# A fourth pair of split buffers for the experts, and five weight pieces of each small expert multiplied in fp32 without a split

## The reference

```
def swiglu(x, w1, w3, w2):
    return (jax.nn.silu(x @ w1) * (x @ w3)) @ w2

def moe_swiglu(x, router_w, w1, w3, w2):
    logits = (t @ router_w)
    top_v, top_i = lax.top_k(logits, TOP_K)          # 2 of 8 experts for each token
    gates = jax.nn.softmax(top_v, axis=-1)
    ...
    for e in range(N_EXPERTS):
        out = out + combine[:, e:e + 1] * swiglu(t, w1[e], w3[e], w2[e])
```

## Time and profile before

| | us |
|---|---|
| median of 3 runs | 2150.57 (2148.72 to 2155.72) |
| the profiled execution | 2145.45 |
| its span in the profile | 2143.6 |
| PE, DVE, ACT busy in it | 1996.8, 1512.1, 1102.2 |
| the eight experts, first to last piece on PE | some 728 to 1781 |

### The profile page before, as it was taken

One profiled execution on the slowest core, in us unless ns is written; L12 is line 12 of the kernel. 1 busy time (PEld: TensorE's weight loads), 2 busy tenths in 40 slices (PEclk: granted clock), 3 DMA queues, 4 the chain that ended last, 5 costly groups with the idle time before them and its releaser, 6 DMA issues.

```text
span 2143.6 us, 25381 instructions
## 1 busy us (share of the span) xinstructions
PE 1996.8 (93%) x9950; PEld 1561.8 (73%) x9950; DVE 1512.1 (71%) x1834; ACT 1102.2 (51%) x1144; POOL 58.2 (3%) x64
## 2 busy tenths in 40 slices
PE   8889999999899899999999898888888898999997
PEld 7578588875695688878878766666666666659997
DVE  4665654457575555568888898989899897646666
ACT  1233243312240344447677687877777782544554
POOL 0120000000400000000000000000000000100000
PEclk9999999999999899999999999999999999999999
DMA  8202254532000766659989899999999994216450
GB/s 331 79 1 80 121 217 172 189 120 109 1 2 2 280 213 212 216 192 370 348 326 375 322 402 355 397 355 393 381 368 403 345 400 145 108 59 255 166 208 20
DMA packets 65019, 484.44 MB, mean 226 GB/s; under 512 B 9840, under 2 KB 12912, under 8 KB 13680
## 3 DMA queue, kind: packets, MB, share of 16 engines
q1 hardware_dynamic: 64880, 482.58, 59.7%
HBM read 481.51 MB, written 1.05 MB: 225 GB/s over the span
## 4 chain that ended last, share of the span: by engine, by line
PE 72%; DVE 13%; issue 7%; ACT 7%; DMA 1%; POOL 1%; SPq 0%; DVEq 0%; ACTq 0%; POOLq 0%
PE bank L622 12%; PE bank L993 11%; PE bank L995 11%; PE bank L994 11%; PE bank L998 7%; PE bank L999 6%; PE bank L825 5%; ACT e_hi L2360 4%; DVE e_lo L1898 4%; PE bank L1017 2%; PE bank L1077 2%; PE bank L629 1%; PE bank L786 1%; DVE b_arena L1413 1%; DVE e_h L1413 1%
## 5 line engine op out<-in xcount | busy, mean ns | idle before, releaser
L1898 DVE TENSOR_TENSOR e_lo<-b_ring,e_hi 128x2048 fp32r<-128x2048 f32 (+1 forms) x407 | 921.4, 2280 | 287.0 <-ACT e_hi L2360 286.1
L2360 ACT ACTIVATE e_hi<-b_ring 128x2048 fp32r<-128x2048 f32 (+1 forms) x407 | 772.1, 1909 | 201.3 <-PE bank L995 111.4
L998 PE MATMUL bank<-e_hi,e_x 128*128 128x512 f32 x672 | 279.8, 416 | 33.0 <-DVE e_lo L1898 23.1
L999 PE MATMUL bank<-e_lo,e_x 128*128 128x512 f32 x672 | 266.1, 396 | 0.0
L993 PE MATMUL bank<-e_hi,e_x 128*128 128x512 f32 (+1 forms) x528 | 208.4, 395 | 4.5 <-DVE e_lo L1898 2.6
L994 PE MATMUL bank<-e_lo,e_x 128*128 128x512 f32 (+1 forms) x528 | 202.9, 384 | 0.0
L995 PE MATMUL bank<-e_hi,e_x 128*128 128x512 f32 (+1 forms) x528 | 202.8, 384 | 0.0
L998 PEld LDWEIGHTS bank<-e_hi,e_x 128*128 128x128 f32 x672 | 127.9, 190 | 100.7 <-DVE e_lo L1898 59.6
L998 PE MATMUL bank<-e_hi,e_th 128*128 128x512 f32 x336 | 137.9, 411 | 20.4 <-DVE e_lo L1898 20.0
L999 PEld LDWEIGHTS bank<-e_lo,e_x 128*128 128x128 f32 x672 | 128.1, 191 | 25.4 <-issue 1.6
L993 PE MATMUL bank<-e_hi,e_th 128*128 128x512 f32 x352 | 137.7, 391 | 0.4 <-DVE e_tl L1902 0.4
(11 more groups left out here) (268 smaller groups left out, 2853.3 us busy)
## 6 DMA issues: line engine op xcount, KB each, us to landing
b_ring<-in_moe_w SPq DMA_DIRECT2D x336, 1024.0 KB, 6.9
b_ring<-in_ffn_w SPq DMA_DIRECT2D x15, 2048.0 KB, 8.3
b_ring<-in_w_in SPq DMA_DIRECT2D x14, 2048.0 KB, 8.4
b_ring<-in_w_up SPq DMA_DIRECT2D x12, 2048.0 KB, 8.3
b_ring<-in_w_down SPq DMA_DIRECT2D x6, 2048.0 KB, 8.6
b_ring<-in_w_o SPq DMA_DIRECT2D x4, 2048.0 KB, 8.3
b_gain<-in_gains SPq DMA_DIRECT2D x6, 1024.0 KB, 4.6
b_ring<-in_w_out SPq DMA_DIRECT2D x2, 2048.0 KB, 8.2
```

The source lines that it names most:

```text
L998: e.matmul(out, both, bh, start=first, stop=False)
L999: return e.matmul(out, both, bl, start=False, stop=last)
L1898: e.tensor_tensor(lo, raw, r32(hi), ALU.subtract).then_inc(lo_dve.sem)
L2360: return e.activation(out, x, ACT.Copy)
```

## The change

- While the experts run, a fourth pair of buffers (`spare_hi`, `spare_lo`) is used: it lies where `gain` and a part of the constants (`masks`) lie at other times. ACT and DVE split three pieces ahead in the experts instead of two (`lead`), and `last_in_place` is p-4 instead of p-3. Three pieces instead of two are split before the first expert.
- In the form "a", the pieces d0 of units 2 to 6 (`WHOLE`; numbers 20, 26, 32, 38 and 40 of an expert) are not split. PE multiplies them as fp32 from the ring, with one matmul where there were two. The half in the ring is then free when PE has finished the piece, not when DVE has its `lo`.
- The load of gain 3 moves from before the experts to their end, and the constants come in two DMAs.

```
@@
+WHOLE = [("d", u, 0) for u in range(2, 7)]
@@
+def whole_pieces(kinds):
+    steps = [x for x in steps_of(FFE_UNITS, 1) if x[0] != "T"]
+    return [i for i, x in enumerate(steps) if kinds == "a" and x in WHOLE]
@@ gated_uses: what frees the halves of a slot
-            halves = {u: ((lo_dve(first + i),), (lo_dve(first + i + 1),)) for i, (u, h, _) in enumerate(ps) if h == 0}
+            kept = {ps[i][0]: [piece(first + i)] for i in whole}
+            halves = {u: (((piece if i in whole else lo_dve)(first + i),), (lo_dve(first + i + 1),)) for i, (u, h, _) in enumerate(ps) if h == 0}
@@
+        def last_in_place(p):
+            if MOE_P <= p < FF2_P:
+                return max(p - NH - 1, MOE_P - 1)
+            return max(p - NH, FF2_P - 1) if p >= FF2_P else p - NH
+
+        def lead(at):
+            return NH if MOE_P <= at < FF2_P else NH - 1
@@ PE
             def two(out, both, bh, bl, first, last):
+                if bl is None:
+                    return e.matmul(out, r32(both), bh, start=first, stop=last)
@@ PE, gated
-                    hi, lo = take_piece(p)
+                    raw = kinds == "a" and (kind, u, hf) in WHOLE
+                    if raw:
+                        e.wait_ge(*pieces[p][0])
+                        hi, lo = pieces[p][1], None
+                    else:
+                        hi, lo = take_piece(p)
@@ DVE, gated (ACT likewise with split_round)
-                        if p + 2 < ends:
-                            split_rest(p + 2)
+                        if p + lead(at) < ends and p + lead(at) - at not in whole:
+                            split_rest(p + lead(at), 1 + (p + lead(at) - 1 - at in whole))
@@ DVE, experts
-                split_rest(MOE_P)
-                split_rest(MOE_P + 1)
+                for i in range(NH):
+                    split_rest(MOE_P + i)
@@ ACT, experts
-                split_round(MOE_P)
-                split_round(MOE_P + 1)
+                e.wait_ge(*ln_out(2))
+                for i in range(NH):
+                    split_round(MOE_P + i)
@@ SP
-            load_gain(3, ln_out(2))
@@ SP, after the loads of the experts
+            load(IN2_AT + 2)
+            load_gain(3, piece(FF2_P - 4))
             load(IN2_AT + 4)
```

More of the change, by code:

```diff
@@ L25 @@
 LEVELS = 7
-CONSTS = ["ident", "ones", "mean256", "tri0", "tri1", "before", "bt0", "bt1", "iota", "pairs", "most"] + \
-    [f"m{d}{k}" for d in range(2) for k in range(LEVELS)] + ["c1", "s1", "c2", "s2"]
+CONSTS = ["ident", "ones", "mean256", "tri0", "tri1", "before", "iota", "pairs", "most", "c1", "s1", "c2", "s2"] + \
+    ["bt0", "bt1"] + [f"m{d}{k}" for d in range(2) for k in range(LEVELS)]
 CWIDTH = {"iota": 256, "most": 8, "c1": 128, "s1": 128, "c2": 128, "s2": 128}
@@ L315, in two_blocks @@
             e_hi, e_lo = ([b[j] for b in split] for j in range(2))
+            moe_hi, moe_lo = ([spare[j], *(b[j] for b in split)] for j in range(2))
         xh2, xl2 = (e_x[:, :, :, 128 * i:128 * i + 128] for i in range(2))
@@ L396, in two_blocks @@
         s_half = [sem(f"half{i}") for i in range(NR)]
-        s_x, s_x1, s_first, s_id, s_c, s_cols, s_rows, s_gain, s_ba, s_pw, s_rw, s_bd, s_out = (
-            sem(n) for n in ("x", "x1", "first", "id", "c", "cols", "rows", "gain", "ba", "pw", "rw", "bd", "out"))
+        s_x, s_x1, s_first, s_id, s_c, s_cols, s_rows, s_gain, s_n1, s_ba, s_pw, s_rw, s_bd, s_out = (
+            sem(n) for n in ("x", "x1", "first", "id", "c", "cols", "rows", "gain", "n1", "ba", "pw", "rw", "bd", "out"))
         def ring_in(n):
@@ L508, in gated_uses @@
                     for i in range(2):
-                        use(tiles_of(i, 1024 * 512 * u, 8, widths[u]), lo_dve(last[k]))
+                        use(tiles_of(i, 1024 * 512 * u, 8, widths[u]), lo_dve(last[k]), *kept.get(k, []))
                         k += 1
@@ L512, in gated_uses @@
                     use(tiles_of(2, 1024 * 512 * (u - 1), widths[u - 1] // 128, 1024),
-                        lo_dve(last[k]))
+                        lo_dve(last[k]), *kept.get(k, []))
                     k += 1
@@ L1002, in take_piece @@
                 e.wait_ge(*lo_dve(p))
-                return e_hi[place(p)], e_lo[place(p)]
+                return hi_of(p), lo_of(p)
             def gated(widths, at, unit, kinds, first=None, aside=None, where=(0, 1)):
@@ L1045, in gated @@
                                     if kinds[s] == "a":
-                                        ins = two(out, e_th[z][:, 2 * hf + c, :], hi[:, cut], lo[:, cut], begin, end)
+                                        ins = two(out, e_th[z][:, 2 * hf + c, :], hi[:, cut], None if raw else lo[:, cut], begin, end)
                                     else:
@@ L1904, in gated @@
             def gated(widths, at, unit, kinds, ends, aside=None):
-                tiles = len(kinds)
+                tiles, whole = len(kinds), whole_pieces(kinds)
                 p, inc = at, 2 // tiles
@@ L2113, in aside @@
                         picks(ex + 1, 0, 2)
-                gated(FFE_UNITS, at, 6 + 7 * ex, kinds, at + 42 + 2 * more, aside)
+                gated(FFE_UNITS, at, 6 + 7 * ex, kinds, at + 42 + lead(at) * more, aside)
                 e.wait_ge(*piece(at + 41))
@@ L2625, in gated @@
                     else:
-                        if p + 2 < ends:
-                            split_round(p + 2)
+                        if p + lead(at) < ends and p + lead(at) - at not in whole:
+                            split_round(p + lead(at), 1 + (p + lead(at) - 1 - at in whole))
                         if kind == "w1" and hf == 1:
```

59 lines of the change are left out of this document (34 added, 25 removed).

## The result

The changed kernel took 2168.28 us (median, 2167.23 to 2171.45) where the kernel before took 2152.07 (2150.57 when the prediction was made, from one run fewer): a ratio of 1.0086, 95% interval 1.0069 to 1.0102, so 16 us slower. The forecast of 2155 and its range to 2167 were too low. The profiled executions are 21.6 us apart in span, 2143.6 and 2165.2. Of this 2.7 us arise before 715 us, in code that the change hardly touches (in the experiments' profiles the same place scatters by 6 us), so the medians are the better figure for the whole and the profiles for where it lies.

What follows compares the result with a forecast made beforehand. A loop through PE, ACT and DVE was taken to bound small experts' units: 0 for it, 3.7 + 1.2 + 0.5 - 1.6 + 1.5 = 5.3 elsewhere, rounded down to +4.5 on 2150.57: 2155, range 2138 to 2167.

Steps and rivals of the forecast that it cites:

- The loop: Small experts' middle units: a gapless chain through PE, ACT and DVE sets 15.46 us, unchanged; +0 to +0.3 per whole-piece unit.
- PE waits at w3.0 for `e_th` as now: Small experts' middle units: PE's wait at w3.0 stays as before, so the unit stays at 15.46 us.
- signs of being wrong: Units under 15 us, w3.0 without a wait, ACT waiting for DMA in small experts, or clock under 1.00 in mid-expert.
- The clock's term: Behind the five expert boundaries: lower clock costs about 1.6 us a stretch, between 0 and 8 in all, taken as +1.5.
- The rival: Lower clock at five boundaries in full, or kept longer by PE's waits at every w3.0: 2162 to 2166, chance 0.20.
- its point of decision: At w3.0: the slower clock case decides where PE's own path, not `e_th`, is the later; 0.9 us of slack.
- Entry: Before the first expert: three splits instead of two ahead of `e_P` delay it by 2.2 to 3.7 us, not given back.
- Boundary: Small experts' unit 5 and boundary: whole pieces add 3.2 us, saved waits offset most; +0.3 each, four times, +1.2.
- turn_picks: One unit per small expert, 0.35 us above the others: PE's part now hidden in waiting, -0.4 four times, -1.6.
- The faster rival: Small experts: work, not the loop, sets the time, so fewer splits shorten units: 2115, or 2135 if half; chance 0.20.

Runs made afterwards that it cites:

- The pairs alone: The changed kernel with no piece in fp32 (`WHOLE = []`), keeping the fourth pair and three splits ahead: 2185.86 us, ratio 1.016.
- the filled run: The changed kernel with two useless fp32 matmuls on PE ahead of the wait at w3.0 of units 2 and 3 (pieces 12 and 18): 2153.48 us.
- the fp32 pieces alone: The changed kernel's five fp32 pieces, but three pairs, a lead of two and two entry splits as in the kernel before: 2154.00 us, ratio 1.0014.
- an opened loop: The changed kernel with `e_th` ahead of the w3.1 split, third entry split behind `e_P`, two idle matmuls before unit 0's T: 2122.94 us; without fp32 pieces 2122.82.
- the order with three pairs: `e_th` put ahead of the split in DVE's order, with three pairs, a lead of two and no fp32 piece: 2196.57 us, ratio 1.0219 to the kernel before.

## Why the prediction was wrong

The loop, the heart of it, held: undisturbed units take 15.45 us with whole pieces as without, DVE's and ACT's 55 and 48 us came as idle time, the loads stayed early enough (the tightest copy in a small expert began 2 us behind its landing), expert forms "na" and "n" didn't move (474.1 us for all three, 474.4 before), and a whole piece costs PE 3.6 us of records.

**The step that failed** is "PE waits at w3.0 for `e_th` as now". It waits for the same thing, but not as long. Before, PE's slack of 2.7 us in a unit (15.46 - 12.7) was spent in portions of up to 1.0 us from start to start, ahead of one `e_lo` after the other, which a lead of two delivers just in time:

```profile
1242.52 0.50 PE L998 MATMUL bank<-e_hi,e_th 128*128 128x512 f32 x1 [0.64 <-DVE e_lo L1898]
1245.32 0.50 PE L998 MATMUL bank<-e_hi,e_x 128*128 128x512 f32 x1 [0.69 <-DVE e_lo L1898]
```

With a lead of three the `e_lo` are there, PE runs through the unit and the whole slack falls on w3.0. I worked PE's slack out as 1.1 us, with a whole piece in the unit; but the first whole piece is number 20, and the waits at pieces 12 and 18 have none before them. There it is 2.5 us. The pairs alone and the filled run show that the loss of the slow middle units, 11 of the 16 us, hangs on this wait. One of the prediction's own signs of being wrong came with it, the clock under 1.00 in the middle of a small expert.

**The clock's term** was mis-sized with it. I took +1.5, at the boundary alone, up to 8. In the profile it is 10.8 us in seven middle units and most of what four of the five starts of an expert lost against the undisturbed 14.87, 11.0 us (they have slow stretches at pieces 0, 1 and 5). The price of one, 1.6 us, was right. The prediction read the lower clock behind one boundary; the trace before has it at three of the five starts (the third is the earlier trace rows):

```profile
1204.30:1207.50 3.20, 3.20 (x9) 2.48 (x8) 1.59 (x2) 1.92 (x1) 0.00 (x0) 0.50 0.92 310
1671.90:1675.10 3.20, 3.20 (x9) 2.55 (x8) 3.20 (x3) 1.91 (x1) 0.00 (x0) 0.50 0.70 210
```

It cost next to nothing there: from piece 0 to w3.0 of unit 1 these three took 16.51 to 16.53 us and the other two 16.37 and 16.39, since only the fast ones then waited for `e_lo`, 1.15 us and 1.19. The fourth pair takes that wait away, as the prediction said, and each slow stretch now counts in full, in four of five starts. The rival had the mechanism, "kept longer because PE now waits at every w3.0", with 2162 to 2166 and a chance of 0.20, but its point of decision (PE's own path being the later at w3.0) was the wrong one: the clock falls where PE is early.

**Entry**: 2.2 to 3.7 predicted, 2.1 seen in the changed kernel's profile and 3.5 to 3.9 in five others. **Boundary**: +0.3 predicted; to the next piece 0 it is +1.1, and behind it -1.5 to -1.7, where no slow stretch takes that back (14.87 us in one expert of five). I had booked the saved wait for `e_lo` ahead of piece 0, but it lies behind it. **turn_picks**: -0.4 predicted, -0.46 measured. **The faster rival** (work sets the time) fell with the fp32 pieces alone, 2154; its 2115 was of the size that an opened loop gives, 2123.

## What to carry to other kernels

Ask of a saved instruction whether it stands in the loop that sets the pace: 25 splits outside it gave nothing, one exchange of two instructions inside gave 38 us against the changed kernel and 19 against the one before. And when a deeper lead removes small waits of PE, add them up, since what isn't gained comes back as one long wait, and behind waits of 1.8 to 2.5 us the clock was often at its lower level. Idle matmuls in such a wait are a cheap test of it, and moving a consumer's last input forward was the cure here.

## What the runs showed of the hardware

Waits of PE of up to 1.4 us inside an expert were followed by a clock of 1.00 (0.83 us in the changed kernel, 1.36 in the order with three pairs), even where they summed to over 4 us in a unit. Waits of 2.5 us at w3.0 were followed by 0.50 for 3 to 4 us in many cases but not in all: in the changed kernel at piece 18 in all five small experts and at piece 12 in two of five, with the same wait; with the pairs alone at pieces 18 and 24 in all five and at piece 12 in none. Waits of 1.8 us did it in places too (piece 30 with the pairs alone). So the length of the one wait does not decide it alone, and what does was not tried. A matmul in fp32 of 512 columns took two records, 3.6 us for a piece of four, and in 30 us of the run with w1.1 in fp32, where PE never waited, the clock was 1.00. The loads went at 392 GB/s over an expert of 112.6 us.
